# A two-layer decoder trunk in float32: TensorE without constant products in its waits at the changes of stage

## The chip, the cores and the metric

The kernel runs on one core of one Trainium2 chip. The metric is the time of one execution on the device in microseconds (us), lower is better. Five engines work side by side: TensorE (PE, whose weight loads are shown apart as PEld), VectorE (DVE), ScalarE (ACT), GpSimd (POOL) and SyncE (SP), which issues most of the DMAs.

## The reference

The input `x` has 256 positions of 2048 features in float32. Two layers follow one another. Each adds three things to the residual `h`, and each of the three is normed before and after:

```python
for i in range(2):
    hn = rms_norm(h, pre_mix_g[i])
    y = conformer_conv(hn, ...) if i == 0 else diff_attention(hn, ...)
    h = h + rms_norm(y, post_mix_g[i])
    f = conv_ffn(rms_norm(h, pre_ffn_g[i]), ...)
    h = h + rms_norm(f, post_ffn_g[i])
    gate = sigmoid(rms_norm(h, ple_pre_g[i]) @ ple_w_gate[i] + ple_b_gate[i])
    h = h + rms_norm(gate * (p[i] @ ple_w_proj[i]), ple_post_g[i])
```

`conformer_conv` is a product to 4096 columns, a gated unit, a causal convolution of width 31, a layer norm, silu and a product back to 2048. `diff_attention` is differential attention with 8 heads. `conv_ffn` goes up to 2 x 5632 features, through a causal convolution of width 3 and a gated silu, and back down.

## The kernel before, in words

Everything is written by hand as one list of instructions for each engine, with semaphores between them; each engine runs its own list in order. The matrices are streamed through a ring of buffers in units of 256 x 512 weights: SP loads a unit (`raw`), ACT casts it to a high part (`w_hi`, L635), DVE makes the low part (`w_lo`, L1048), and PE multiplies. A product of float32 accuracy is made of three products of high and low parts. In the stages whose results stay as rows by token (down, gates, v, wo, pw2) these are L1728, L1729 and L1730 in `half_unit`; in the stages that make rows by feature (up, qk) they are L1701 and L1703 in `feature_chunk`, which cover the three in two instructions.

Between two stages lies a turn. When the last chunk of a stage is made, ACT squares it (L673), DVE forms the mean square (L1064, L1066), POOL takes the inverse root (`rstd`, L567), and DVE adds the normed result to the residual: four pieces of 128 x 256 first (`residual_begun`, L1104), the others behind them (L1095). PE turns the new `h` from rows by token to rows by feature, with transposes against the identity: `turn_begun` (L1657) for the first four blocks of `h`, `turn_h` (L1673) for the others, called from within the next stage. ACT scales the turned tiles into the high part of `x` (L665), DVE makes their low part (L1075), and after the first two of those `feature_chunk` may begin.

Three turns are of interest, named after what is added to `h`: mix0 (after the convolution module of layer 0, before its up stage), ple0 (after the embedding of layer 0, before the qk stage) and mix1 (after the attention of layer 1, before its up stage). In these PE has nothing of the reference to do for a while. There, and once before all else, it runs the helper `keep_warm(n, bank)` (L1787 to L1790): n products of the identity with itself, into a PSUM bank that the next real product overwrites. Nobody waits for them, and they signal nothing. The counts are in L91: six at the beginning (L1793); at mix0 15 and at mix1 13 between the wait for the first two pieces of the moved result and the wait for all eight (L1990), then four behind `turn_begun` (L1993); at ple0 three ahead of `turn_begun` (L1907) and four behind it (L1910).

The waits at mix0 and mix1 are these, in PE's list:

```python
pe.wait_ge(mix_moved, PIECES * layer + HALVES)
keep_warm(MIX_WARM[layer], 0)
pe.wait_ge(mix_moved, PIECES * (layer + 1))
turn_begun(f"mix{layer}")
keep_warm(TURN_WARM[1], 0)
```

Of the kernel before, what the change touches and what calls it, by code (L numbers as in the profile page):

```python
# [67 lines left out]
def trunk(nc, t, out):  # L68
# [19 lines left out]
    CH_GLU, CH_FFN, CH_QK = D // PAIR_N, FF // PAIR_N, D // PAIR_N  # L88
    ACT_PAIRS = 5
    PE_TAPS = 14  # L90
    WARM_UP, MIX_WARM, TURN_WARM = 6, (15, 13), (3, 4)  # L91
    QUICK = {"mix0": 0, "ple0": 1, "mix1": 2}
    ALONE = ("ffn0", "mix1", "ffn1")
    GRING = 12
# [171 lines left out]
    with ctx:  # L266
# [157 lines left out]
        def load_constants(engine, which):  # L424

            n = 0
            for g, (parts, _, _, _) in enumerate(groups):
                row = 0
                for _, src in parts:
                    if consts_loader(n) == which:  # L430
                        engine.dma_start(const_rows[row:row + src.shape[0], g], src).then_inc(consts_landed[which], 16)
                    row += src.shape[0]
                    n += 1
# [192 lines left out]
        def _(act):  # L626
# [92 lines left out]
            def keep_columns(some):  # L719
                for g in some:  # L720
                    _, rows, of, first = groups[g]
                    act.wait_ge(cols_turned, g + 1 if g < 2 else len(groups))
                    dst = {"cols": cols, "conv": wconv}[of]
                    bank, at = column_bank(g)
                    nc.scalar.copy(dst[:, first:first + rows], ps[:, bank, at:at + rows]).then_inc(cols_ready, 1)
# [906 lines left out]
        def _(pe):  # L1632
# [14 lines left out]
            def turn_begun(add):  # L1647


                for q in range(UNIT_N // PAIR_N):  # L1650
                    for half in range(HALVES):
                        if q:
                            pe.wait_ge(h_updated, PIECES * ADD[add] + half + 1)
                        else:
                            pe.wait_ge(h_begun, HALVES * QUICK[add] + half + 1)
                        for kt in (2 * q, 2 * q + 1):
                            ins = nc.tensor.transpose(tiles[:, turned_at(BECOMES[add], kt), P * half:P * (half + 1)],  # L1657
                                                      h[:, half, P * kt:P * (kt + 1)], ident[:])
                    ins.then_inc(turned, 1)
# [127 lines left out]
            def keep_warm(n, bank):  # L1787

                for _ in range(n):
                    mm(ps[:, bank, 0:P], ident[:], ident[:], start=True, stop=True)  # L1790
# [108 lines left out]
            for layer in range(DEPTH):  # L1899
                if layer == 1:  # L1900
# [3 lines left out]
                        pe.wait_ge(biased, PIECES + 2 * (c + 1))  # L1904
                        token_unit(u, lambda half: ps[:, 2 * c + half], (0, 1), p_x, True, True)
                    pe.wait_ge(biased, 2 * PIECES)
                    keep_warm(TURN_WARM[0], 4)  # L1907
                    turn_begun("ple0")
                    pe.wait_ge(early_ready, EARLY[0] + EARLY[1])
                    keep_warm(TURN_WARM[1], 0)  # L1910

                    def between_qk(j):
                        turn_rest("ple0", j)
# [73 lines left out]
                        token_chunk(i, place["wo"] + UPC, lambda half: ps[:, (i + 1) * HALVES + half])  # L1987

                pe.wait_ge(mix_moved, PIECES * layer + HALVES)
                keep_warm(MIX_WARM[layer], 0)  # L1990
                pe.wait_ge(mix_moved, PIECES * (layer + 1))
                turn_begun(f"mix{layer}")
                keep_warm(TURN_WARM[1], 0)  # L1993

                def first_chunk(j):

# [86 lines left out]
```

## Time and profile before

| | |
|---|---|
| median of three runs | 2409.73 us (2409.35 to 2409.79) |
| the profiled execution | 2409.29 us |
| its span, first to last instruction | 2407.5 us |
| PE busy | 2398.4 us, 12370 products |
| DVE busy | 1638.7 us |
| ACT busy | 1210.6 us |
| DMA | 452.49 MB, mean 188 GB/s |

The span is shorter than the execution's time by 1.8 us that lie around the instructions. A float32 product on the identity shows as two passes on PE, a transpose as one. PE's passes overlap, so the durations of single passes are longer than the distance from one to the next.

### The profile page before, as it was taken

To read this page: it belongs to the slowest core of one execution; us is meant where nothing else is said; L and a number is where in the kernel's file an instruction comes from. 1 tells how busy PE (TensorE), PEld (TensorE's weight loads), DVE (VectorE), ACT (ScalarE), POOL (GpSimd) and SP (SyncE) were. 2 spreads that over 40 slices of the span, in tenths; PEclk is the share of its full clock that TensorE was granted. 3 is DMA by queue.
4 is the path that set the end of the run, shared out by engine and by line. 5 is a ranking of instruction groups with operands and counts; after the bars stand their busy time and mean duration, and the time that the engine had idled before them with its cause. 6 is when DMAs were issued, how large, how long until landed. Compare 5 with 4: busy or idle time off the path is not lost.

```text
span 2407.5 us, 38755 instructions
## 1 busy us (share of the span) xinstructions
PE 2398.4 (100%) x12370; PEld 2058.2 (85%) x12370; DVE 1638.7 (68%) x2229; ACT 1210.6 (50%) x1755; POOL 36.0 (1%) x66
## 2 busy tenths in 40 slices
PE   9999999999999999999999999999999999999999
PEld 8888788888888888888888888888888888888887
DVE  6999767777777754447755677477777777644475
ACT  3433655555555544446644455465555555444464
POOL 2000000000000000000000000000000000000000
PEclk9999999999999999999999999999999999999999
DMA  8552546656656665556566544556566656655564
GB/s 269 182 164 92 175 158 199 188 180 197 192 183 191 194 209 194 193 196 226 180 215 202 180 149 156 195 162 191 182 193 192 187 180 200 210 193 195 193 230 150
DMA packets 370943, 452.49 MB, mean 188 GB/s; under 512 B 27460, under 2 KB 279494, under 8 KB 369440
## 3 DMA queue, kind: packets, MB, share of 16 engines
q1 hardware_dynamic: 367456, 435.54, 55.7%
q0 software_dynamic: 2960, 15.02, 1.9%
q8 instruction: 44, 0.72, 0.1%
q10 hardware_dynamic: 432, 0.79, 0.1%
q14 instruction: 51, 0.42, 0.1%
HBM read 447.05 MB, written 4.19 MB: 187 GB/s over the span
## 4 chain that ended last, share of the span: by engine, by line
PE 98%; SPq 0%; DVE 0%; issue 0%; DMA 0%; ACT 0%; POOL 0%; DVEq 0%; POOLq 0%; ACTq 0%
PE ps L1701 32%; PE ps L1703 16%; PE ps L1730 13%; PE ps L1728 13%; PE ps L1729 13%; PE ps L1783 9%; PE ps L1673 1%; PE ps L1949 0%; PE ps L1935 0%; SPq L478 0%; PE ps L1876 0%; PE ps L1790 0%; DMA h<-in_x 0%; PE ps L1884 0%; PE ps L1657 0%
## 5 line engine op out<-in xcount | busy, mean ns | idle before, releaser
L1048 DVE TENSOR_TENSOR w_lo<-raw,w_hi 128x1024 fp32r<-128x1024 f32 x758 | 923.7, 1223 | 622.3 <-ACT w_hi L635 619.8
L635 ACT CAST w_hi<-raw 128x1024 fp32r<-128x1024 f32 x758 | 791.4, 1049 | 734.9 <-PE ps L1730 366.1
L1701 PE MATMUL ps<-x,w_hi 128*128 128x512 f32 x3328 | 1155.8, 392 | 0.0
L1703 PE MATMUL ps<-x,w_lo 128*128 128x256 f32 x3328 | 931.5, 280 | 0.0
L1701 PEld LDWEIGHTS ps<-x,w_hi 128*128 128x128 f32 x3328 | 622.4, 187 | 136.2
L1703 PEld LDWEIGHTS ps<-x,w_lo 128*128 128x128 f32 x3328 | 628.9, 189 | 0.0
L1730 PE MATMUL ps<-w_hi,mid 128*128 128x512 f32 x704 | 273.9, 389 | 0.0
L1729 PE MATMUL ps<-w_lo,mid 128*128 128x512 f32 x704 | 273.9, 389 | 0.0
L1728 PE MATMUL ps<-w_hi,mid 128*128 128x512 f32 x704 | 273.9, 389 | 0.0
L1728 PE MATMUL ps<-w_hi,x 128*128 128x512 f32 x640 | 253.2, 396 | 0.0
L1730 PE MATMUL ps<-w_hi,x 128*128 128x512 f32 x640 | 249.2, 389 | 0.0
L1729 PE MATMUL ps<-w_lo,x 128*128 128x512 f32 x640 | 249.1, 389 | 0.0
L1783 PE MATMUL ps<-xn,wg 128*128 128x256 f32 x896 | 193.7, 379 | 0.0
L1783 PEld LDWEIGHTS ps<-xn,wg 128*128 128x128 f32 x896 | 170.2, 190 | 23.1
L1503 DVE SCALAR_TENSOR_TENSOR acc<-ext,cols,acc 128x256 f32<-128x256 f32 x352 | 147.2, 480 | 45.6 <-ACT acc L952 39.3
L1728 PEld LDWEIGHTS ps<-w_hi,mid 128*128 128x128 f32 x704 | 132.2, 188 | 27.4
L1729 PEld LDWEIGHTS ps<-w_lo,mid 128*128 128x128 f32 x704 | 132.2, 188 | 27.4
L1730 PEld LDWEIGHTS ps<-w_hi,mid 128*128 128x128 f32 x704 | 132.2, 188 | 27.4
L1730 PEld LDWEIGHTS ps<-w_hi,x 128*128 128x128 f32 x640 | 120.1, 188 | 25.3
L1728 PEld LDWEIGHTS ps<-w_hi,x 128*128 128x128 f32 x640 | 120.2, 188 | 24.9 <-issue 0.5
L1729 PEld LDWEIGHTS ps<-w_lo,x 128*128 128x128 f32 x640 | 120.2, 188 | 24.6 <-issue 0.2
L1241 DVE SCALAR_TENSOR_TENSOR acc<-u_ext,wconv,acc 128x256 f32<-128x256 f32 x322 | 133.8, 476 | 1.2 <-ACT acc L769 1.1
(202 smaller groups left out, 1274.0 us busy)
## 6 DMA issues: line engine op xcount, KB each, us to landing
raw<-in_ffn_w_in SPq DMA_DIRECT2D x704, 256.0 KB, 3.1
raw<-in_ffn_w_out SPq DMA_DIRECT2D x352, 256.0 KB, 3.4
raw<-in_attn_w_qkv SPq DMA_DIRECT2D x192, 256.0 KB, 2.9
raw<-in_ple_w_gate SPq DMA_DIRECT2D x128, 256.0 KB, 3.7
wg<-in_conv_w_pw SPq DMA_DIRECT2D x112, 256.0 KB, 3.9
raw<-in_conv_w_pw SPq DMA_DIRECT2D x64, 256.0 KB, 3.6
raw<-in_attn_w_o SPq DMA_DIRECT2D x64, 256.0 KB, 3.5
wg<-in_conv_w_pw SPq DMA_DIRECT2D x32, 128.0 KB, 4.1
```

The source lines that it names most:

```text
L635: nc.scalar.copy(w_hi[:, u % RING], raw[:, u % RING]).then_inc(hi_split, 1)
L1048: nc.vector.tensor_tensor(w_lo[:, u % RING], raw[:, u % RING], w_hi[:, u % RING].bitcast(F32), ALU.subtract).then_inc(split_done, 1)
L1241: step.mark(nc.vector.scalar_tensor_tensor(both[:, a], u_ext[:, p, tap:tap + T], wconv[:, tap * KT + p:tap * KT + p + 1], nshift[:] if tap ...
L1503: ins = nc.vector.scalar_tensor_tensor(acc[:, f], ext[:, f, tap:tap + T], col(f"ffn_tap{layer}{tap}", c * 2 + (f if f < 2 else FT + f - 2) ...
L1673: ins = nc.tensor.transpose(tiles[:, turned_at(left, kt), P * half:P * (half + 1)], h[:, half, P * kt:P * (kt + 1)], ident[:])
L1701: mm(ps[:, 4 * s + f], w_hi[:, u % RING, q, columns], x[:, kt].rearrange("p a t -> p (a t)"), start=kt == 0, stop=False)
L1703: ins = mm(ps[:, 4 * s + f, 0:T], w_lo[:, u % RING, q, columns], x[:, kt, 0], start=False, stop=kt == KT - 1)
L1728: mm(bank(half), hi, w_hi[:, u % RING, q], start=first, stop=False)
L1729: mm(bank(half), hi, w_lo[:, u % RING, q], start=False, stop=False)
L1730: ins = mm(bank(half), lo, w_hi[:, u % RING, q], start=False, stop=last)
L1783: ins = mm(ps[:, 4 * (c % 2) + f, 0:T], wg[:, glu_slot(u), q, P * f:P * (f + 1)], source[:, kt], start=kt == 0, stop=kt == KT - 1)
```

## The change

The counts of the products at the three turns go away, and with them their five calls. All waits stay where they are. The six products at the beginning stay.

```diff
-    WARM_UP, MIX_WARM, TURN_WARM = 6, (15, 13), (3, 4)
+    WARM_UP = 6
...
                     pe.wait_ge(biased, 2 * PIECES)
-                    keep_warm(TURN_WARM[0], 4)
                     turn_begun("ple0")
                     pe.wait_ge(early_ready, EARLY[0] + EARLY[1])
-                    keep_warm(TURN_WARM[1], 0)
...
                 pe.wait_ge(mix_moved, PIECES * layer + HALVES)
-                keep_warm(MIX_WARM[layer], 0)
                 pe.wait_ge(mix_moved, PIECES * (layer + 1))
                 turn_begun(f"mix{layer}")
-                keep_warm(TURN_WARM[1], 0)
```

## Rows read from the trace of the kernel before

**Rows 1.** The page: span, busy time of PE, granted clock by slices, chain by engine.
```profile
span 2407.5 us, 38755 instructions
...
PE 2398.4 (100%) x12370; PEld 2058.2 (85%) x12370; DVE 1638.7 (68%) x2229; ACT 1210.6 (50%) x1755; POOL 36.0 (1%) x66
...
PEclk9999999999999999999999999999999999999999
...
PE 98%; SPq 0%; DVE 0%; issue 0%; DMA 0%; ACT 0%; POOL 0%; DVEq 0%; POOLq 0%; ACTq 0%
```

**Rows 2.** Line 1790: duration in ns, least, median and most; first and last start.
```profile
L1790 PE MATMUL ps<-ident x98: 270/275/580, 1.5 to 1570.6; 128*128 128x128 f32 x98
```

**Rows 3.** Waits of PE: us in total, times, longest.
```profile
PE ps L1790 <- POOL minus_half L552: 1.5, 1, 1.5
...
PE ps L1657 <- DVE h L1104: 0.2, 1, 0.2
```

**Rows 4.** Timeline at mix0: start, us (of the whole group), engine, line.
```profile
340.93 0.39 PE L1730 MATMUL ps<-w_hi,x 128*128 128x512 f32 x1
...
341.16 3.51 PE L1790 MATMUL ps<-ident 128*128 128x128 f32 x30
...
344.25 1.67 DVE L1104 SCALAR_TENSOR_TENSOR h<-y_mix,rstd,h 128x256 f32<-128x256 f32 x4 [0.35 <-POOL rstd L567]
...
344.88 1.53 PE L1657 MATMUL ps<-ident,h 128*128 128x128 f32 x8 [0.21 <-DVE h L1104]
...
346.17 0.88 DVE L1075 SCALAR_TENSOR_TENSOR x<-ps,cols,x 128x256 fp32r<-128x256 f32 x2 [0.24 <-ACT x L665]
346.25 1.06 PE L1790 MATMUL ps<-ident 128*128 128x128 f32 x8
...
347.11 0.19 PEld L1701 LDWEIGHTS ps<-x,w_hi 128*128 128x128 f32 x1
347.14 0.47 PE L1701 MATMUL ps<-x,w_hi 128*128 128x512 f32 x1
```

**Rows 5.** Timeline at ple0.
```profile
1179.61 0.39 PE L1730 MATMUL ps<-w_hi,p_x 128*128 128x512 f32 x1
...
1179.81 1.67 DVE L1104 SCALAR_TENSOR_TENSOR h<-z,rstd,h 128x256 f32<-128x256 f32 x4 [0.66 <-POOL rstd L567]
1179.84 0.83 PE L1790 MATMUL ps<-ident 128*128 128x128 f32 x6
...
1180.51 1.47 PE L1657 MATMUL ps<-ident,h 128*128 128x128 f32 x8
...
1182.71 0.47 PE L1701 MATMUL ps<-x,w_hi 128*128 128x512 f32 x1
```

**Rows 6.** Timeline at mix1.
```profile
1565.11 0.39 PE L1730 MATMUL ps<-w_hi,x 128*128 128x512 f32 x1
...
1565.33 3.06 PE L1790 MATMUL ps<-ident 128*128 128x128 f32 x26
...
1568.42 1.53 PE L1657 MATMUL ps<-ident,h 128*128 128x128 f32 x8
...
1570.68 0.47 PE L1701 MATMUL ps<-x,w_hi 128*128 128x512 f32 x1
```

**Rows 7.** Line 1790 in two stretches: busy us (instructions), granted clock, DMA share, GB/s.
```profile
1.50:3.00 1.50, 1.47 (x7) 1.47 (x8) 1.00 0.42 124
...
341.50:343.00 1.50, 1.50 (x16) 1.50 (x15) 1.00 0.00 1
```

**Rows 8.** Timeline of PE at the beginning.
```profile
1.53 2.93 PE L1790 MATMUL ps<-ident 128*128 128x128 f32 x12 [1.53 <-POOL minus_half L552]
...
7.02 1.99 PE L1783 MATMUL ps<-x,wg 128*128 128x256 f32 x8 [0.53 <-DVE x L1187]
```

**Rows 9.** PE at the end: last group of the timeline, then stretches with the granted clock.
```profile
2401.94 1.12 PE L2058 MATMUL ps<-z,diag 128*128 128x512 f32 x2
...
2405.40:2405.60 0.20, 0.00 (x0) 1.00 1.02 389
2405.60:2405.80 0.20, 0.00 (x0) 0.50 1.07 389
```

## The prediction

> **What bounds the kernel now.** I read the page first. TensorE (PE) is busy for 2398.4 us of a span of 2407.5 us, and the chain that ended last lies on PE for 98% of its length [rows 1]. So time saved or lost in dense PE work goes one for one into the end. Then I read the line that the change takes away, L1790. It has 98 passes on PE, two for each of 49 products [rows 2]; twelve are the six products at the start, which stay, and 86 passes (43 products) go: 30 and 8 at the turn after the mixer of layer 0, 6 and 8 at the turn after the embedding of layer 0, 26 and 8 at the turn after the mixer of layer 1 [rows 4 to 6]. Nobody waits for any of them: they write a PSUM bank that the next real product starts over, and signal nothing.
>
> The list of PE's waits holds only two that matter here: 1.5 us at the very start and 0.2 us for h (L1104), at the turns [rows 3]. That list hides the real waits. At each turn PE must wait until the residual h is made by VectorE and until the first x is split, and the constant products lie in just these waits. The timeline shows how long they are. At mix0 the last real product ends at 340.93 + 0.39 = 341.32 us and the first transpose of h begins at 344.88: 3.56 us with nothing real to do. The transposes take until 346.41, and the dense work of the next stage (L1701) begins at 347.14 [rows 4]. At ple0 the same three times are 1180.00, 1180.51 and 1182.71 [rows 5]. At mix1 they are 1565.50, 1568.42 and 1570.68 [rows 6]. From real product to dense work that is 5.8, 2.7 and 5.2 us, with eight transposes in each.
>
> **What the removal gives directly.** The question at each turn is whether PE waits for its own constant products or for VectorE. At mix0 the first h piece is one quarter of the four-piece group at 344.25 (1.67 / 4 = 0.42 us), so it is there at 344.67. The 30 passes end at 344.67 too, and the transposes start 0.21 us later; at ple0 h is there at 1180.23, the transposes start 0.28 us later, with the six passes ending at 1180.67. At worst ple0's first transpose is held by 0.07 us, and since VectorE paces the four h pieces, it isn't passed on. After the transposes the x parts of VectorE end at 346.17 + 0.88 = 347.05, and the first weight load of L1701 starts at 347.11, 0.06 us behind [rows 4]; the eight passes also end just then, so which of the two held it can't be read. The other two turns show the same (0.07 us each). So the direct gain is bounded by 0 below and 3 x 0.07 = 0.2 us above. I take 0.1 us. The other queues lose nothing: no DMA, wait or semaphore moves, and ScalarE, VectorE, GpSimd and SP run the same lists.
>
> **What it may cost: PE's clock.** PE has two levels, 1.2 and 2.4 GHz, and the trace shows both. At the start the same product on the identity ran at half pace: 8 weight loads in 1.5 us against 15 in 1.5 us at the turn [rows 7]. All twelve passes at the start, from 1.53 to 4.46 us, are at this pace, and the products of L1783 at 7.02 us (8 in 1.99 us) are at full pace [rows 8] (the granted clock is printed as 1.00 there, so before its first change that column is no evidence; the pace is). From an idle PE to full clock, the start thus shows a stretch of 2.9 to 5.5 us. In the other direction the end of the span has the price: the last PE pass ends at 2401.94 + 1.12 = 2403.06, and the granted clock falls from 1.00 to 0.50 at 2405.6, 2.5 us later [rows 9]. Nothing else in the span shows a fall; the page has PEclk at its top in all slices [rows 1].
>
> Now put that on the turns with their constant products gone. Mix0 leaves PE without any pass for 3.56 us and mix1 for 2.92 us: both longer than the 2.5 us after which the clock fell at the end. Ple0 leaves 0.51 us, and about 0.7 us more behind its transposes: shorter. So I expect the clock to fall at two of the three turns.
>
> The price of one fall. While the clock is at half, PE does half the work, so each us of dense work under it costs 0.5 us. If the way back is counted from the first transpose, as it was from the first pass at the start, it ends 2.9 to 5.5 us after 344.88, at 347.8 to 350.4. Dense work begins at 347.14, so 0.6 to 3.2 us of it are at half clock: 0.3 to 1.6 us lost. The transposes before it are paced by VectorE, so only the last two of the eight show, with 0.11 us more each (pace 0.1 to 0.2 us a pass, [rows 7]): 0.2 us. That makes 0.5 to 1.8 us. If the fall comes later, only once the transposes are running, the whole way back lies in dense work: up to 5.5 / 2 = 2.75 us. The lower end of all this is 0, the upper 2.75 us; I take 1.4 us, between the ends of the likelier case and nearer its top because the later fall pulls that way. The same for mix1 (its gap between transposes and dense work is 2.3 us as at mix0).
>
> Can it be made up later? No: behind each turn PE waits for nothing in the list [rows 3], so the 1.4 us isn't taken out of any later wait; VectorE and ScalarE only get further ahead.
>
> **Sum**, against the profiled execution (2409.29 us, of which the span is 2407.5): -0.1 + 2 x 1.4 = +2.7 us, so 2412.0. The median of the three runs shown is 2409.73, 0.44 us above the profiled one, so 2412.4 is the forecast for the median. That is +0.11%. Since about 0.2% (4.8 us) is what a measurement of this kernel can tell from no change, the forecast is called no change, though I believe the sign to be a loss.
>
> **Rivals.**
> 1. *The clock doesn't fall, or at one turn only.* A fall needs the transposes (from 344.88 and 1568.42) to come too late to hold it. The single fall in the trace came behind the very end, with nothing following; for mix1 the margin over 2.5 us is only 0.4 us. None: -0.1 us, median 2409.6. One: +1.3, median 2411.0. For it: the margins; against it: both gaps are longer than the one measured. Chance 0.2 (none 0.07, one 0.13).
> 2. *It falls at all three turns.* If the transposes don't hold the clock up, what counts is the stretch from real product to dense work: 5.8, 2.7 and 5.2 us, all longer than 2.5 us. Then 3 x 1.4 - 0.1 = +4.1 us, median 2413.8. For it: ple0's 2.7 us; against it: that is over 2.5 us by 0.2 only, and no row shows what transposes alone do. Chance 0.15. The Trainium skill, page "TensorE: Matmul & The Clock Gate", Part 4 (PE-mode transpose), says that the full clock does not engage for transposes. No row of this trace has transposes alone long enough to show it; by that rule this rival would be the case.
> 3. *Slower by more than 0.2%.* The mechanism is the length of the way back: at each turn the fall comes late, so that dense work pays all 5.5 us. Two turns give 5.5 us (median 2415.1), three 8.25 us (2417.9). It decides from 2.4 us a turn at two turns, or 1.6 us at three. For it: at 1.6 us the three-turn case is near; against it: it needs the upper bound twice, and the clock at the start was back at some time before 7.02. Chance 0.12, part of it from rival 2 with a higher price.
> 4. *The removal frees PE and is faster.* It would need constant products that hold real work; the rows allow 0.2 us in all. To reach 4.8 us is not possible by them. Chance 0.02, for what no row shows.
>
> **How the numbers follow.** Two falls at about 1.4 us: 0.51, the likeliest, and the predicted time is its own: 2412.4. The range takes in the case of no fall at its low end (2409.6) and two falls at the full price at its high end (2415.1, and 0.4 for the spread of runs: 2415.5); what is left out is three falls at a high price and any faster result, about 1 in 10 together. Faster by over 0.2% 0.02; within 0.2% 0.86; slower 0.12.
>
> **What would show it.** Right: in the changed kernel the timeline has no PE pass between 341.3 and 344.9 (nor between 1565.5 and 1568.4); the granted clock reads 0.50 in windows there and in the first us of L1701; the pair L1701, L1703 is spaced at about 0.7 us instead of 0.35 for up to 3 us; ple0 reads 1.00; and from 352 us on every line of layer 0 is later by the same 1 to 2 us, then by twice that after the turn of mix1. The start of the transposes after h, and of x after them, stays within 0.1 us. Wrong: the clock at 1.00 in all three turns; or a loss that shows where the clock is full (a wait for split weights or x in the stage behind a turn); or first transposes that start clearly earlier than 0.21 us after h.

## The result and the profile after

The changed kernel takes 2414.29 us (median of 15 runs, 2412.78 to 2415.94) against 2409.73 for the kernel before (15 runs, 2408.94 to 2410.78): a ratio of 1.0018, 95% interval 1.0011 to 1.0025. It is slower by 4.56 us, 0.19%. The forecast was 2412.4 with a range of 2409.6 to 2415.5. (A few executions of the kernel before and of the experiments took more than 3400 us for a reason that nothing here shows; they are left out of the ranges and counts below.)

The page of the changed kernel has a little less work for PE and a longer span. Its clock row of 40 slices shows nines throughout, as in [rows 1]: a slice is 60 us, too coarse for what follows.

```profile
span 2411.0 us, 38585 instructions
...
PE 2392.7 (99%) x12284; PEld 2050.9 (85%) x12284; DVE 1639.7 (68%) x2229; ACT 1211.3 (50%) x1755; POOL 36.1 (1%) x66
```

86 passes fewer (12370 to 12284), PE 5.7 us less busy, and the span 3.5 us longer. PE's waits now show what the constant products covered, the wait for h at all three turns (compare [rows 3]):

```profile
PE ps L1657 <- DVE h L1104: 6.9, 3, 3.6
...
PE ps L1701 <- issue: 1.4, 2, 0.7
...
PE ps L1701 <- DVE x L1075: 0.9, 1, 0.9
```

The timeline of PE at mix0, to be held against [rows 4]:

```profile
341.03 0.39 PE L1730 MATMUL ps<-w_hi,x 128*128 128x512 f32 x1
344.98 1.94 PE L1657 MATMUL ps<-ident,h 128*128 128x128 f32 x8 [3.56 <-DVE h L1104]
347.59 0.76 PE L1701 MATMUL ps<-x,w_hi 128*128 128x512 f32 x1 [0.67 <-issue]
...
348.37 0.63 PE L1701 MATMUL ps<-x,w_hi 128*128 128x512 f32 x1
...
349.01 0.63 PE L1701 MATMUL ps<-x,w_hi 128*128 128x512 f32 x1
...
351.19 0.39 PE L1701 MATMUL ps<-x,w_hi 128*128 128x512 f32 x1
...
351.54 0.40 PE L1701 MATMUL ps<-x,w_hi 128*128 128x512 f32 x1
```

The last real product and the first transpose are each 0.10 us later than before, which this execution had already lost ahead of the turn: the transposes start no earlier without the constant products. But they take 1.94 us in place of 1.53, L1701 follows 2.61 us behind their start in place of 2.26, and its pairs are 0.64 us apart (348.37 to 349.01) where they are 0.35 us apart at full clock (351.19 to 351.54). At mix1:

```profile
1566.96 0.39 PE L1730 MATMUL ps<-w_hi,x 128*128 128x512 f32 x1
1570.27 1.54 PE L1657 MATMUL ps<-ident,h 128*128 128x128 f32 x8 [2.92 <-DVE h L1104]
1572.54 0.62 PE L1701 MATMUL ps<-x,w_hi 128*128 128x512 f32 x1 [0.73 <-issue]
```

Here the transposes ran at full clock, as in [rows 6], and only L1701 is slow. The granted clock in stretches (columns: from and to, length, PE busy with its instructions, granted clock, DMA share, GB/s; 1.00 is 2.4 GHz, 0.50 is 1.2 GHz) says where it fell and where it was back:

```profile
343.00:343.50 0.50, 0.00 (x0) 1.00 0.00 0
344.50:350.50 6.00, 4.85 (x17) 0.50 0.00 1
351.00:352.00 1.00, 1.00 (x9) 1.00 0.07 8
1180.00:1190.00 10.00, 8.67 (x50) 1.00 0.42 156
1572.00:1573.00 1.00, 0.46 (x2) 0.85 0.00 0
1573.00:1576.00 3.00, 3.00 (x11) 0.50 0.00 0
1576.50:1577.50 1.00, 1.00 (x9) 1.00 0.00 0
```

It is at half from between 343.5 and 344.5 to between 350.5 and 351, and again from 1572.7 (0.85 over one us is 0.3 us at half) to a little behind 1576; ple0 (1180 to 1190) keeps 1.00. To see what each turn cost, I take the distances between the start of the last real product ahead of one turn and that ahead of the next (341.03, 1181.46, 1566.96 and the end at 2411.0 for the changed kernel; 341.01, 1182.58, 1569.72 and 2413.7 for its second profile; before, [rows 4 to 6] and the span):

| from, to | before | changed | changed, second profile |
|---|---|---|---|
| last L1730 ahead of mix0 to the one ahead of ple0 | 838.68 | 840.43 (+1.75) | 841.57 (+2.89) |
| ahead of ple0 to ahead of mix1 | 385.50 | 385.50 (0) | 387.14 (+1.64) |
| ahead of mix1 to the end of the span | 842.39 | 844.04 (+1.65) | 843.98 (+1.59) |

The first two columns explain +3.4 of the +3.5 us between the two profiled executions. (At ple0 L1701 started 0.15 us late, and this was gone before mix1.) But this profiled execution, 2412.78 us, was the fastest of the 15. The second profile is that of experiment 7.

### The profile page after: what moved, and what is told of

Read it like the earlier page. It is cut to its first block, busy times and chain, and to the rows that moved or that the text cites. A ratio compares the mean times of both kernels' runs of the same rounds, so it can differ in the third digit from the quotient of the medians.

```text
span 2411.0 us, 38585 instructions
## 1 busy us (share of the span) xinstructions
PE 2392.7 (99%) x12284; PEld 2050.9 (85%) x12284; DVE 1639.7 (68%) x2229; ACT 1211.3 (50%) x1755; POOL 36.1 (1%) x66
## 4 chain that ended last, share of the span: by engine, by line
PE 98%; DVE 1%; issue 0%; SPq 0%; DMA 0%; ACT 0%; POOL 0%; DVEq 0%; POOLq 0%; ACTq 0%
PE ps L1701 32%; PE ps L1703 16%; PE ps L1728 13%; PE ps L1730 13%; PE ps L1729 13%; PE ps L1783 9%; PE ps L1673 1%; PE ps L1947 0%; PE ps L1933 0%; SPq L478 0%; PE ps L1876 0%; DMA h<-in_x 0%; PE ps L1884 0%; PE ps L1657 0%; SPq L495 0%
## 5 line engine op out<-in xcount | busy, mean ns | idle before, releaser
L1701 PE MATMUL ps<-x,w_hi 128*128 128x512 f32 x3328 | 1158.6, 392 | 2.3 <-issue 1.4
L1703 PE MATMUL ps<-x,w_lo 128*128 128x256 f32 x3328 | 932.7, 280 | 0.0
L1701 PEld LDWEIGHTS ps<-x,w_hi 128*128 128x128 f32 x3328 | 623.8, 187 | 139.9 <-issue 3.1
L1703 PEld LDWEIGHTS ps<-x,w_lo 128*128 128x128 f32 x3328 | 630.3, 189 | 0.0
L1730 PE MATMUL ps<-w_hi,mid 128*128 128x512 f32 x704 | 273.9, 389 | 0.0
L1728 PE MATMUL ps<-w_hi,mid 128*128 128x512 f32 x704 | 273.9, 389 | 0.0
L1728 PE MATMUL ps<-w_hi,x 128*128 128x512 f32 x640 | 253.3, 396 | 0.0
L1730 PE MATMUL ps<-w_hi,x 128*128 128x512 f32 x640 | 249.3, 389 | 0.0
L1783 PE MATMUL ps<-xn,wg 128*128 128x256 f32 x896 | 193.7, 379 | 0.0
L1783 PEld LDWEIGHTS ps<-xn,wg 128*128 128x128 f32 x896 | 170.2, 190 | 23.1
L1728 PEld LDWEIGHTS ps<-w_hi,mid 128*128 128x128 f32 x704 | 132.2, 188 | 27.7
L1730 PEld LDWEIGHTS ps<-w_hi,mid 128*128 128x128 f32 x704 | 132.2, 188 | 27.2
L1730 PEld LDWEIGHTS ps<-w_hi,x 128*128 128x128 f32 x640 | 120.1, 188 | 25.5
L1728 PEld LDWEIGHTS ps<-w_hi,x 128*128 128x128 f32 x640 | 120.2, 188 | 24.9 <-issue 0.7
```

The lines of the kernel that those rows point to most:

```text
L1701: mm(ps[:, 4 * s + f], w_hi[:, u % RING, q, columns], x[:, kt].rearrange("p a t -> p (a t)"), start=kt == 0, stop=False)
L1703: ins = mm(ps[:, 4 * s + f, 0:T], w_lo[:, u % RING, q, columns], x[:, kt, 0], start=False, stop=kt == KT - 1)
L1728: mm(bank(half), hi, w_hi[:, u % RING, q], start=first, stop=False)
L1730: ins = mm(bank(half), lo, w_hi[:, u % RING, q], start=False, stop=last)
L1783: ins = mm(ps[:, 4 * (c % 2) + f, 0:T], wg[:, glu_slot(u), q, P * f:P * (f + 1)], source[:, kt], start=kt == 0, stop=kt == KT - 1)
```

## The experiments

Two theories stood against each other at first. *Clock*: the loss is dense work at half clock after the turns. *Restart*: an engine that was idle starts late, whatever the clock. And within the clock theory it was open which turns take part, and whether transposes hold the clock up. All edits are shown against the kernel before, with `...` for lines left out, except that of experiment 8.

**1. Only the products ahead of the transposes at mix0 and mix1.**

```diff
-                    keep_warm(TURN_WARM[0], 4)
                     turn_begun("ple0")
...
-                    keep_warm(TURN_WARM[1], 0)
...
                 turn_begun(f"mix{layer}")
-                keep_warm(TURN_WARM[1], 0)
```

> The products between the two waits at mix0 and mix1 (15 and 13) are kept, the four behind the transposes and both calls at ple0 are removed. Clock theory (the loss is time at half clock after PE had nothing to do at mix0 and mix1): PE is idle only about 0.7 us behind each set of transposes, the clock stays at 1.00, the median is that of the kernel before within 0.5 us, so 2409.5 to 2410.3. Restart theory (an idle PE starts late, whatever the clock): each of three restarts of L1701 costs 0.15 us or more, so about 2410.2 or above at full clock. If transposes do not hold the clock, the stretch from the last constant product to L1701 is about 2.5 us, as long as the one before the fall at the end of the span, and a fall at mix0 or mix1 in some executions would give a wide spread, 2410 to 2412.

Measured 2410.21 us against 2410.16 (1.0001, 0.9992 to 1.0010); the eleven runs lie between 2409.27 and 2411.32.

```profile
341.00:352.00 11.00, 10.05 (x70) 1.00 0.09 27
1180.00:1190.00 10.00, 8.67 (x52) 1.00 0.51 183
1565.00:1576.00 11.00, 10.25 (x70) 1.00 0.25 79
```

The clock is at 1.00 at all three turns, and at the two mix turns L1701 starts 2.27 us behind the transposes:

```profile
345.34 1.53 PE L1657 MATMUL ps<-ident,h 128*128 128x128 f32 x8 [0.22 <-DVE h L1104]
347.61 0.47 PE L1701 MATMUL ps<-x,w_hi 128*128 128x512 f32 x1 [0.73 <-issue]
```

That is 0.01 us more than in [rows 4]. The longer gap was already in the changed kernel: at mix1, where its transposes ran at full clock, the first of them follows 3.31 us behind the start of the last real product (1566.96 to 1570.27) after 2.92 us idle, as it does in [rows 6]. So an idle PE at full clock restarts at no cost at the mix turns, and the restart theory falls for them. The four products behind the transposes do nothing that can be measured once those ahead are there.

**2. Only the products ahead of the transposes at mix0 and mix1 removed.**

```diff
                 pe.wait_ge(mix_moved, PIECES * layer + HALVES)
-                keep_warm(MIX_WARM[layer], 0)
                 pe.wait_ge(mix_moved, PIECES * (layer + 1))
```

> Only the 15 and 13 products at mix0 and mix1 are removed; the four behind the transposes and both calls at ple0 are kept. Clock theory: PE is idle 3.6 and 2.9 us there, the clock falls at both, and the four products under half clock take twice their time and push L1701 back a little: 2412.5 to 2414.5, no better than the changed kernel by more than 1.5 us. Rival (the four products behind the transposes are what matters, since the gap behind the transposes is the one in which the clock falls at mix1): 2409.7 to 2411.

Measured 2412.45 against 2410.16 (1.0009, 1.0000 to 1.0018), at the lower edge of what was expected.

```profile
246.00:249.00 3.00, 3.00 (x4) 0.50 0.00 0
344.00:344.50 0.50, 0.00 (x0) 1.00 0.00 0
345.50:351.50 6.00, 6.00 (x25) 0.50 0.01 1
352.00:353.00 1.00, 1.00 (x8) 1.00 0.35 75
1568.00:1575.00 7.00, 4.08 (x26) 1.00 0.31 98
```

The clock fell at mix0 and not at mix1: I had expected both. The four products behind the transposes lie in the very place where it fell at mix1 in the changed kernel. One profile can't show that they prevent it. The mean granted clock of each execution, on record to three places, says more: it is 0.999 in eight of the eleven runs here and 0.998 in three, and 0.996 or 0.997 in all 26 runs of the changed kernel (15 and the 11 of experiment 7). I estimate from this at most 7.2 us at half clock in those eight, in all of the span, and 12 us or more in each of the 26. So with these products at the three turns PE spends less time at half clock; at which turn it is saved in each execution isn't shown. There is also a fall that nobody had foreseen, by 246 us, in the layer norm of layer 0, a part that this experiment leaves as it is.

**3. Only the products at ple0 removed.**

```diff
-                    keep_warm(TURN_WARM[0], 4)
                     turn_begun("ple0")
                     pe.wait_ge(early_ready, EARLY[0] + EARLY[1])
-                    keep_warm(TURN_WARM[1], 0)
```

> Only the two calls at ple0 are removed. Clock theory: 0.4 us idle before and 0.7 us behind the transposes, clock at 1.00 in every execution, median within 0.3 us of the kernel before (2409.5 to 2410.0), L1701 there about 0.15 us later. Rival (transposes do not hold the clock and the 2.7 us there is enough for a fall in some executions): a fall costs 1.4 us or more, so a median of up to 2411.2 or a spread wider than that of the kernel before by 1.5 us.

Measured 2409.89 against 2410.16 (0.9999, 0.9990 to 1.0008), eleven runs from 2409.44 to 2410.74, clock 1.00 in the profile:

```profile
1180.00:1190.00 10.00, 8.66 (x51) 1.00 0.46 166
```

No sign of a fall at ple0 in these runs: the slowest is 0.85 us above the median, less than the 1.6 us that a fall at a turn costs in the table. (Two of the eleven have a mean clock of 0.999, as some of the kernel before have; see experiment 11.)

The beginning of this profile does show something. The twelve passes of L1790 at 1.54 us take 2.93 us as in [rows 8], but the first eight passes of L1783, 1.99 us there, take almost twice that:

```profile
7.04 3.63 PE L1783 MATMUL ps<-x,wg 128*128 128x256 f32 x8 [0.20 <-DVE x L1187]
```

PE's pace was thus at half until about 10.5 us, and in experiment 1 too (3.76 us for the same passes). In experiment 8 the transposes at 4.84 us already run at full pace (8 in 1.09 us). The code at the beginning is the same in all of these, so the first way up, counted from the first pass, took anything from about 3 to 9 us.

**4. Transposes in place of products.** Twice as many, since a product is two passes and a transpose one.

```diff
                 for _ in range(n):
-                    mm(ps[:, bank, 0:P], ident[:], ident[:], start=True, stop=True)
+                    if bank == 2:
+                        mm(ps[:, bank, 0:P], ident[:], ident[:], start=True, stop=True)
+                    else:
+                        for _ in range(2):
+                            nc.tensor.transpose(ps[:, bank, 0:P], ident[:], ident[:])
```

> At all three turns each constant product (two passes) is replaced by two transposes of the identity (one pass each), so that PE is as busy as in the kernel before but with transposes alone. If transposes hold the clock as products do: clock 1.00, 2409.5 to 2410.0. If they do not: the clock falls at mix0 and mix1 as in the changed kernel and at ple0 perhaps, 2412.5 to 2416.

Measured 2409.96 against 2410.16 (1.0000, 0.9991 to 1.0009), runs from 2409.61 to 2411.18. The transposes at mix0 (L1794 here) and the granted clock at the three turns:

```profile
341.68 3.44 PE L1794 MATMUL ps<-ident 128*128 128x128 f32 x30
```

```profile
341.00:348.00 7.00, 6.71 (x52) 1.00 0.12 42
1180.00:1184.00 4.00, 4.00 (x29) 1.00 0.27 113
1565.00:1572.00 7.00, 6.91 (x51) 1.00 0.41 128
```

Float32 transposes hold the clock at all three turns as products do. The Trainium skill, page "TensorE: Matmul & The Clock Gate", Part 4 (PE-mode transpose), says that the full clock does not engage for transposes. These runs speak against it for float32 transposes and a clock that is already up; whether transposes alone would bring it up from half no run here shows.

**5. and 6. One mix turn at a time.** All products removed at mix0 alone, then at mix1 alone:

```diff
-    WARM_UP, MIX_WARM, TURN_WARM = 6, (15, 13), (3, 4)
+    WARM_UP, MIX_WARM, TURN_WARM = 6, (0, 13), (3, 4)
...
-                keep_warm(TURN_WARM[1], 0)
+                keep_warm(TURN_WARM[1] * layer, 0)
```

```diff
-    WARM_UP, MIX_WARM, TURN_WARM = 6, (15, 13), (3, 4)
+    WARM_UP, MIX_WARM, TURN_WARM = 6, (15, 0), (3, 4)
...
-                keep_warm(TURN_WARM[1], 0)
+                keep_warm(TURN_WARM[1] * (1 - layer), 0)
```

> Only the products at mix0 (15 and 4) are removed; ple0 and mix1 as in the kernel before. In the changed kernel's profile the clock was at half from 343.9 to 350.8 us there. Clock theory: a fall at mix0 in every execution, PE at half clock for at least the first 3 us of L1701, +1.5 to +3 us against the kernel before (2411.6 to 2413.2), more than half of what the whole change costs (4.6 us). The one with all the cost at mix1 would give +0.3 or less.

> Only the products at mix1 (13 and 4) are removed. The gap there is shorter (2.9 us instead of 3.6), and in the run that kept the four products behind the transposes the clock did not fall at it. Clock theory: a fall in most executions but perhaps not in all, +0.8 to +2 us against the kernel before (2410.9 to 2412.1), with this and the run without mix0's products adding up to the whole change, +4 to +5 us. If both together give clearly less than 4 us, part of the loss comes from ple0 or from doing several at once.

Mix0 alone: 2412.21 against 2409.81 (1.0011, 1.0002 to 1.0019). Mix1 alone: 2412.48 against the same (1.0010, 1.0001 to 1.0019). That is +2.4 and +2.7 us, 5.1 together. (In the profile of the first, the distance from mix0 to ple0 grew by 1.64 us, 342.06 to 1182.38; another 1.1 us was lost ahead of mix0, where nothing was changed.) Mix1 costs more than I expected from the shorter gap. In its profile the clock fell ahead of the transposes (the first of these stretches is 0.93), where in the changed kernel's it fell after L1701 had begun:

```profile
1568.00:1568.50 0.50, 0.00 (x0) 0.93 1.04 361
1569.00:1575.00 6.00, 5.30 (x19) 0.50 0.01 3
1575.50:1576.50 1.00, 1.00 (x10) 1.00 0.00 0
```

From the last real product (1565.73) to the end of its span (2410.2) it took 844.47 us, 2.08 more than before: a fall at the same turn had cost 1.65 in the changed kernel.

**7. The changed kernel once more.** No edit.

> The changed kernel once more, for a second profiled execution and beside the others on one chip. If the cost of a fall depends on where in the turn the clock falls and comes back, the falls of this execution lie elsewhere than at 343.9 and 1572.7 us or last longer or shorter, and its time differs from 2412.8 by what the half-clock time of L1701 differs, halved. Median 2413.7 to 2415. If the fall is tied to the gap itself, both lie at the same distance from the last real product as before, 2.5 and 5.4 us.

Measured 2415.11 against 2409.81 (1.0021, 1.0012 to 1.0030): +5.3 us, about as much as experiments 5 and 6 together, and 0.1 us above what was expected. Its profiled execution took 2415.46 us, and is the last column of the table above.

```profile
346.50:347.00 0.50, 0.00 (x0) 0.51 0.00 0
347.00:353.50 6.50, 6.27 (x22) 0.51 0.25 80
353.50:354.50 1.00, 1.00 (x10) 1.00 0.04 14
1186.00:1186.50 0.50, 0.50 (x3) 0.68 1.13 475
1187.00:1190.00 3.00, 3.00 (x12) 0.57 0.48 170
1190.50:1191.50 1.00, 1.00 (x11) 1.00 0.74 239
1575.00:1575.50 0.50, 0.20 (x1) 0.80 0.00 0
1576.00:1579.00 3.00, 3.00 (x12) 0.55 0.00 0
```

(A value between 0.50 and 1.00 is a stretch that the half clock covers in part: 0.51 in the first row puts the fall at 346.5, 0.68 puts the one at ple0 at 1186.2, 0.80 the one at mix1 at 1575.3.) The same program, and the falls lie elsewhere. At mix0 the clock is still full while the transposes run and falls as they end, so that all dense work from L1701's start at 347.23 to 353.3 is at half clock, 6.1 us: +2.89 us in place of +1.75. At ple0 it falls 0.35 us after L1701 has begun (1185.83), in a turn that kept 1.00 in the first profile: +1.64 us. The time lost follows from how much dense work lies under the half clock, and this differs from one execution to the next. The sum of the last column is 6.1 us, and the spans differ by 6.2.

Read in steps of 0.1 us, the falls ahead of the end of the span have two lengths only. The half clock lasted 6.8 us at mix0 in all five profiles where it fell (the changed kernel, 343.9 to 350.8, and experiments 2, 5, 7 and 8) and at mix1 in experiment 6 (1568.4 to 1575.3): in all of these it fell before L1701 began. It lasted 3.4 us where it fell as L1701 began or later (mix1 in the changed kernel, 1572.7 to 1576.2, and in experiments 7 and 8; ple0 here), and in the layer norm in experiments 2 and 8. A pair of L1701 and L1703 takes 0.64 us in place of 0.35 at half clock, so 0.45 us are lost for each us of dense work under it: 3.4 us make 1.5, and 6.1 us make 2.8, close to the 1.6 and 2.9 of the table.

**8. Four products at each mix turn.** Eight passes in place of 30 and 26; nothing behind the transposes and nothing at ple0. Against the changed kernel:

```diff
-    WARM_UP = 6
+    WARM_UP, MIX_WARM, TURN_WARM = 6, (4, 4), (3, 4)
...
                 pe.wait_ge(mix_moved, PIECES * layer + HALVES)
+                keep_warm(MIX_WARM[layer], 0)
                 pe.wait_ge(mix_moved, PIECES * (layer + 1))
```

> Four products (8 passes, 0.9 us) at mix0 and mix1 in place of 15 and 13, nothing behind the transposes and nothing at ple0. PE is then idle 2.6 and 2.0 us before the transposes and 0.7 us behind. If the fall needs an idle stretch of 2.5 us or more: none at mix1, one in some executions at mix0, 2410 to 2411.5. If the falls need only that PE is little busy around the turn: falls at both, 2412 to 2414.

Measured 2412.96 against 2409.81 (1.0014, 1.0005 to 1.0022), and falls at both:

```profile
345.00:345.50 0.50, 0.00 (x0) 1.00 0.00 0
346.00:352.50 6.50, 5.77 (x20) 0.50 0.00 1
...
1574.00:1574.50 0.50, 0.50 (x3) 1.00 0.00 0
1575.00:1578.00 3.00, 3.00 (x11) 0.50 0.02 5
```

The timeline has PE's longest idle stretch at mix1 ahead of the transposes, in brackets:

```profile
1571.71 1.53 PE L1657 MATMUL ps<-ident,h 128*128 128x128 f32 x8 [2.03 <-DVE h L1104]
```

It was idle there for no longer than 2.03 us at a time, and the clock fell all the same. So my measure, the 2.5 us of idle time behind which it fell at the end of the span [rows 9], is no bound below which a gap is safe.

**9. The layer norm's waits filled too**, since the clock had fallen there, at 246 to 247 us, in the profiles of experiments 2 and 8. From the last statistics (L1854) to the first product of the next stage (L1728) those took 10.03 and 10.02 us (244.23 to 254.26, 244.83 to 254.85) against 9.01 before (244.58 to 253.59).

```diff
             ins.then_inc(pe_taps, 1)
+            keep_warm(4, 7)
             stats_of(PAIRS - 1).then_inc(moments, 1)
...
             project_early(0, 0)
+            keep_warm(2, 7)
             spread_statistic(7, 2)
```

> The kernel before, with four more constant products in PE's wait ahead of the last statistics of the layer norm (1.05 us idle at 243.6) and two ahead of the statistic behind the first early projection (0.4 us idle at 247.9), into bank 7, free there. In the profiles of two experiments the clock fell at 246 to 247 us, in a stage that no experiment touched, and cost 1.0 us between the statistics and the first product of the next stage. Clock theory: these falls happen in some executions of the kernel before too; with the products they don't, so the median is 2409.5 to 2409.9, lower than that of the kernel before by 0 to 0.5 us, and the slowest runs are closer to the median (before: up to 1.5 us above it). If the products are late for the wait they cost up to 0.2 us.

Measured 2409.77 against 2409.86 (0.9999, 0.9989 to 1.0008), runs from 2409.21 to 2410.21. It is not told apart from the kernel before. One of the ten runs has a mean clock of 0.999, against six of the 20 of the kernel before beside them; that points the right way, but ten runs don't prove it. Inconclusive.

**10. Eight products more at each mix turn.**

```diff
-    WARM_UP, MIX_WARM, TURN_WARM = 6, (15, 13), (3, 4)
+    WARM_UP, MIX_WARM, TURN_WARM = 6, (23, 21), (3, 4)
```

> 23 and 21 constant products at mix0 and mix1 in place of 15 and 13: 16 passes more at each, 0.11 us apart at full clock, 1.76 us. The 15 and 13 end just when h is there, so if constant products cost only what does not fit into the wait, PE's transposes come 1.7 us later at each turn and the median is 3.0 to 3.6 us above that of the kernel before, clock 1.00. If the next stage makes some of it up (VectorE and ScalarE being further ahead), less, down to 0.

Measured 2412.84 against 2409.86 (1.0013, 1.0004 to 1.0022): +3.0 us at the lower edge of what was expected.

```profile
341.26 0.39 PE L1730 MATMUL ps<-w_hi,x 128*128 128x512 f32 x1
...
341.49 5.29 PE L1790 MATMUL ps<-ident 128*128 128x128 f32 x46
346.62 1.04 PE L1657 MATMUL ps<-ident,h 128*128 128x128 f32 x8
...
348.74 0.47 PE L1701 MATMUL ps<-x,w_hi 128*128 128x512 f32 x1 [0.19 <-issue]
```

From the last real product to L1701 it is 7.48 us in place of 6.21: the 1.76 us of further passes come out as 1.27, since the transposes, no longer paced by h, run in 1.04 us. At mix1 it is 1.24 us (1566.99 to 1573.80, 6.81 us in place of 5.57). The two make 2.5 of the 3.0 us; where the rest is lost I did not follow. Constant products are free only as far as the wait reaches. With 15 and 13 they end just with it.

**11. The kernel before once more**, for a second profile.

> The kernel before once more, for a second profile. At the three turns the clock stays at 1.00. At 246 us it may fall: in two of eight profiles of the experiments it did; if it does here, the span is longer by about 1.0 us and the same group of early projections takes 3.2 to 3.7 us in place of 1.96.

2409.58 us, clock 1.00 at all turns, and no fall at 246 us. A fall in the layer norm is thus seen only in the profiles of experiments 2 and 8. But the mean clocks show that the kernel before has falls too: of its 34 executions beside experiments 5 to 8, eight have 0.999, with a median of 2410.77 us, and 26 have 1.000, with a median of 2409.70. A mean of 0.999 is, as an estimate, 2.4 us or more at half clock. The 1.1 us fit the 1.0 us that the layer norm took longer in experiments 2 and 8; where these falls lie isn't shown.

The end of this profile is worth a look beside [rows 9]. PE's last passes start at 2402.24 and take 1.12 us, and behind them:

```profile
2403.40:2407.80 4.40, 0.00 (x0) 1.00 0.77 285
```

PE had nothing to do for 4.4 us and the clock stayed up, where the first profile of the same kernel had it fall after 2.5 us, and experiment 8 after two idle stretches of 2.03 and 0.73 us. The length of the idle stretch alone doesn't say whether the clock falls.

## Why the prediction came out as it did

**What bounds the kernel** held: PE without slack behind each turn, so that what dense work loses reaches the end. The table's parts add up to the spans.

**The direct gain** (0.1 us, bounds 0 and 0.2) was nothing. The first transpose at mix0 stands 3.95 us behind the start of the last real product in both kernels (340.93 to 344.88, 341.03 to 344.98), and L1701 in experiment 1 follows at the same distance. VectorE held both, not the constant products. At ple0 the first transpose came 0.07 us sooner (0.83 in place of 0.90 us), just the 0.07 us that I had named there, and as I had said it wasn't passed on.

**That the clock falls at mix0 and mix1** held, in both profiles of the changed kernel, and experiments 5 and 6 show that each does its part alone. The ground I gave for it did not: the 2.5 us from the end of the span were seen once, and the same kernel's second profile has 4.4 us idle at full clock (experiment 11).

**The price of one fall** is the term that was mis-sized. I took 1.4 us, from 0.5 to 1.8 if the clock fell before the transposes and up to 2.75 if it fell later. Measured in the profiles with nothing at the turn were 1.75, 2.89 and 1.64 at mix0 and 1.65, 1.59 and 2.08 at mix1, and 2.4 and 2.7 as the medians with one turn bare. The step that failed is the counting of the way back from the first transpose, as if PE's restart began it: at mix0 the clock was at half for 6.8 us in both profiles, from a point that moved by 2.6 us, and in the second 6.1 us of it lay in dense work. The start of the span [rows 7, 8] showed how long the first way up took in one execution; experiments 1 and 3 took until about 10.5 us, so its 2.9 to 5.5 us were no bounds. The rate was a little smaller than assumed, 0.45 in place of 0.5 us for each us of dense work. The half-clock transposes cost 0.35 us in place of the 0.2 assumed.

**That ple0 keeps its clock** held in one profile and not in the other, where it cost 1.64 us. Rival 2 was given 0.15, by transposes that don't hold the clock up. Its outcome happened in one of the two profiled executions, its reason fell with experiment 4: transposes without gaps do hold it. What was wrong in my step for ple0 is the rule of 2.5 us idle, which experiments 8 and 11 refute: several shorter idle stretches around a few transposes can do it as well. How often ple0 falls stays open. It had no constant products in five profiles (the changed kernel twice, experiments 1, 3 and 8) and fell in one. The difference of the medians, 5.3 us in experiment 7 against 5.1 us for the mix turns alone, would leave it little, but each of these medians is uncertain by about 2 us.

**Sum.** Two falls at the measured medians, 2.4 + 2.7 = 5.1 us, against the 2.8 us forecast; the loss measured in the two comparisons is 4.56 and 5.3 us. That the median lies within the range is in part luck: the upper end of 2415.5 came from a way back of 5.5 us that no run bears out as a bound, and five of the changed kernel's 26 executions lie above it. The forecast of no change by the 0.2% bound held narrowly in the first comparison (0.19%) and would have missed in the second (ratio 1.0021).

## What to carry to other kernels

Work that nobody waits for can still be on the critical path by what it keeps up: before it is taken out of TensorE's waits, look at how little PE would do from the last dense work to the next, transposes and short waits included, and reckon 1.6 to 2.9 us of loss (as measured here) for each turn where the clock falls. Fill such a wait to its end and no further: four products in place of 15 and 13 left 3.2 of 5.3 us of loss, and eight more than fit at two turns cost 3.0 us of the 3.5 that they last. A loss like this varies from one execution to the next, so take two profiles and the median of many runs; the first profile here was the fastest of fifteen. And don't take a bound from one event of one profile: the prediction took two in that way, 2.5 us of idleness to a fall and 5.5 us at most to the way back, and later profiles contradict both.

## What was not expected of the hardware

- Float32 transposes of the identity keep TensorE at its full clock as well as products do (experiment 4: 1.00 at all three turns).
- The clock fell with PE idle for only 2.03 us at a time (experiment 8), and at ple0 with 0.45 us idle ahead of the transposes and 0.89 us behind them (experiment 7), in one of five profiles. It stayed up over 4.4 us with PE idle at the end of experiment 11.
- The half clock lasted 3.4 or 6.8 us in every one of the twelve falls ahead of the end of a span, and nothing between.
- It can fall after dense work has resumed: at 1572.7 us, when L1701 had begun at 1572.54. Such a fall costs as much (1.65 us) as one in the gap, since it is the dense work behind it that pays.
